# Another order of work around the last head of an attention and in the first block of a Strassen MLP

## The chip, the cores and the metric

The kernel runs on one core of a Trainium2 chip. The metric is the device time of one execution in microseconds; the median of the runs is given. The engines are called TensorE (PE, with PEld for its weight loads), VectorE (DVE), ScalarE (ACT), GpSimd (POOL) and SyncE (SP). Here SyncE issues all large DMAs, in order: a wait of one DMA holds back all that are written behind it.

## The reference, cut to what matters

One layer of a transformer on 2048 rows of 1024 numbers in f32: differential attention with 8 heads, then an MLP of width 4096 with a squared ReLU.

```python
u = rms_norm(h, norm1_g)
q, k, v = split(u @ w_in, 3)                      # 8 heads, two maps of width 64 each, v of width 128
p = softmax(where(mask, q @ k.T * scale, -inf))   # for both maps; chunk-causal mask
pd = p[:, :, 0] - lam * p[:, :, 1]
o = rms_norm(pd @ v, sub_g) * (1 - lambda_init)
h = h + o @ w_out
u = rms_norm(h, norm2_g)
h = h + square(relu(u @ mlp_w1)) @ mlp_w2
```

## The kernel before

All products are made from f32 numbers split into a high part (f32r) and a low part, three matmuls for each product. There are three stages.

The attention is 128 steps, a = 0 to 127: head h = a // 16, row block j = a % 16 of 128 rows. A step makes the scores of block a, turns (transposes) the probabilities of block a - 1 and multiplies them with v. Up to head 6 it also projects q, k and v of block a + 16. In the last head no projection is left; its place is taken by the output product. Step j there works on output tile t = j - 4: it multiplies the turned attention outputs of row block t with w_out (`pe_product(t, d, parts)`: two column halves d, each in two parts of 12 matmuls), adds x (`dve_residual`, L821), squares the row (`act_square_h`, L829), norms it (`dve_norm_u2`, L846), turns it in the next step (`pe_turn_u2`) and splits it into the seven factors of the MLP's Strassen product. For an odd tile of a pair these are sums and differences: `turned_u2` makes two factors and the sums themselves (L940 to L949, ScalarE's copy L913), `sums_u2` the last three factors (L891 on ScalarE, L926 on VectorE). So only steps with even t have `sums_u2`, of tile t - 1. Meanwhile the outputs of row block t + 1 are loaded (`load_o`, L743), turned (`pe_turn_o`, L772) and split (`turned_o`: L780 on ScalarE, L787 on VectorE) for the next step's product.

Steps with j = 8 to 15 are written in `big_step` of each engine (t = 4 to 11 in the last head), those below in `small_step`. After step 127 a tail, written out by hand, does output tiles 12 to 15.

The order on each engine is the order in the program; engines wait for each other by semaphores. All turned blocks pass through two PSUM slots in the order of `turn_order()`. A transpose waits until its slot's last user is read (`wait_slot`). In a big step the order is u0, u1, p0, p1, ..., o0, o1, so p0 takes the slot of u0. Both halves of the output product up to tile 12 share one PSUM bank: the second half d = 1 waits for the residual of the first (`h_set`, 2t + 1).

The order of TensorE's big step in the last head is: scores of map 0, late values of block a - 2, product half 0, turned u of tile t - 1, scores of map 1, p0, half of product half 1, p1, the other half, then values and p2, p3, then the outputs of block t + 1. ScalarE's order there is: exponentials of map 0, turned u, p0, p1, exponentials of map 1 with p2 and p3 between and behind, the norm of an output, sums of u, turned outputs, square of h.

The MLP is 16 blocks: two chunks of 1024 rows by eight blocks of 512 hidden columns. A block has seven "up" products of 24 matmuls (L2102), which give the hidden values in four quarters, and seven "down" products of 24 (L2126), which are added to y (L2027). ScalarE makes the high parts of the 14 weight factors (`high_w`, L1922) and of the hidden factors (`high_a`, L1935), keeps products (`keep`, L1941), applies relu (L1947) and square (L1951). VectorE makes the low parts of w1's factors (`low_w1`, L2003) and of the hidden factors (`low_a`, L2008), and puts products together (`put_together`, L2015). GpSimd makes the low parts of w2's factors (`low_w2`, L1877) and most weight sums (`weight_sum`, L1790). Up product p = 3 waits for the first `put_together`, p = 4 for `keep` of p = 2. In the first block (`it` = 0) the last output tile's work (`last_tile`) is done between the MLP's own steps, and GpSimd's first weight sums, the first two weights' splits (`high_first_w1` L1679, `low_first_w1` L1683) lie at the end of the attention.

Of the kernel before, what the change touches and what calls it, by code (L numbers as in the profile page):

```python
# [19 lines left out]
P = 128  # L20
# [3 lines left out]
NT = S // P  # L24
# [195 lines left out]
def attention_engines(nc, ctx, x, norm1_g, w_in, q_g, k_g, lambdas, w_out, sub_g, norm2_g, o_dram, u_dram,  # L220
# [5 lines left out]
    def sem(name):  # L226
        return ctx.enter_context(nc.semaphore(name))
# [82 lines left out]
    def staged(pair, o, part):  # L310
# [42 lines left out]
    w_out_loaded = [sem("w_out_loaded0"), sem("w_out_loaded1")]  # L353
    w_out_hi_set, w_out_lo_set = sem("w_out_hi_set"), sem("w_out_lo_set")
    g2_loaded = sem("g2_loaded")
    o_loaded, o_turned, ot_hi_set, ot_lo_set = (
        sem("o_loaded"), sem("o_turned"), sem("ot_hi_set"), sem("ot_lo_set"))
    xr_loaded = [sem("xr_loaded0"), sem("xr_loaded1")]
    multiplied, h_set, h_squared = sem("multiplied"), sem("h_set"), sem("h_squared")
    h_var_set, h_rs_set, u2_normed, u2_turned = (  # L360
# [366 lines left out]
    def low_w_out(engine, kt):  # L727
        engine.wait_ge(w_out_hi_set, kt + 1)
        engine.tensor_tensor(w_out_lo[:, kt, :], w_out_raw[:, kt, :], w_out_hi[:, kt, :].bitcast(F32),
                             ALU.subtract).then_inc(w_out_lo_set, 1)  # L730

    def load_o(sp, t):
        if t == 0:
            for n in range(4):
                sp.wait_ge(w_lo_set[n], H)
            sp.wait_ge(proj_half, 2 * ALL)
            sp.dma_start(g2_row[:, :], norm2_g.to_broadcast([P, D])).then_inc(g2_loaded, 16)
        else:
            sp.wait_ge(o_turned, 2 * t)
        a = ALL - NT + t if t < NT - 2 else ALL - 2 * NT + t  # L740
        cols = slice(0, D if t < NT - 2 else D - HD)
        sp.wait_ge(o_stored[a % 2], 16 * (a // 2 + 1))
        sp.dma_start(o_in[:, cols], o_dram[t * P:(t + 1) * P, cols]).then_inc(o_loaded, 16)  # L743

    def load_x(sp, t):
        if t >= 2:
# [4 lines left out]
    def store_h(sp, t):  # L751
        sp.wait_ge(h_set, 2 * t + 2)
        sp.dma_start(h_dram[t * P:(t + 1) * P, :], xh[:, t % 2, :]).then_inc(h_stored[t % 2], 16)
# [6 lines left out]
            sp.dma_start(factor[pair % 4], stage(pair, o).bitcast(F32)).then_inc(u2_stored[STAGE[pair, o][0]], 16)  # L760

    def pe_turn_o(pe, t):
        pe.wait_ge(o_loaded, 16 * (t + 1))
        for n in range(2):
            wait_slot(pe, "o", t, n)
            for c in range(HALF):
                kt = n * HALF + c
                rows = o_in[:, kt * P:(kt + 1) * P]
                if t >= NT - 2 and kt == KT - 1:
                    pe.wait_ge(o_normed, ALL - NT + t + 1)  # L770
                    rows = o_sum[:, t % 2, :]
                last = pe.transpose(turn[:, slot_of("o", t, n), c * P:(c + 1) * P], rows, ident[:, :])  # L772
            last.then_inc(o_turned, 1)
# [182 lines left out]
    def sync(sp):  # L956
# [44 lines left out]
                store_output(sp, a - 2)  # L1001

        for t in range(NT - OUT0, NT):
            store_h(sp, t - 1)
            if t + 1 < NT:
                load_o(sp, t + 1)
            if t + 1 < NT:
                load_x(sp, t + 1)
            if t == NT - 3:
                sp.wait_ge(pv_done, groups_through(ALL - 1))  # L1010
                mlp.load_first_w1(sp)
            store_u2(sp, t - 1)
            if t == NT - 3:
                sp.wait_ge(scored, scores_through(ALL - 1))
                for place in range(11):
                    sp.wait_ge(u2_stored[place], 16 * staged_through(CT - 1, place))
                for n in range(3):
                    mlp.load_u(sp, 0, n)
            if t == NT - 2:
                for place in (0, 2, 4, 6):  # L1020
                    sp.wait_ge(u2_stored[place], 16 * STAGED[place])
                for n in range(3, 5):
                    mlp.load_u(sp, 0, n)
# [83 lines left out]
    def scalar(act):  # L1107
# [102 lines left out]
        def big_step(a, n, nb):  # L1210
            h, j = split(a)
            t = output_tile(h, j)
            np = count_of(j)
            if j > BIG:
                act_output_low(act, a - 2)
            for k in range(np):
                act_exp(act, a, 0, k)
            if n - 1 < ALL:
                act_turned_qk(act, n - 1)
            if j > BIG:  # L1220
                act_square_output(act, a - 2)
            if t >= 1:
                act_turned_u2(act, t - 1)
            if j == NT - 1 and h + 2 < H:
                act_split_weights(act, h + 2, (0, 1))
            act_turned_p(act, a - 1, 0)
            if nb > 1:
                act_turned_p(act, a - 1, 1)
            act_exp(act, a, 1, 0)
            if n < ALL:  # L1230
                act_keep_qkv(act, n)
            if nb > 2:
                act_turned_p(act, a - 1, 2)
            act_exp(act, a, 1, 1)
            if nb > 3:
                act_turned_p(act, a - 1, 3)
            if n < ALL:
                act_square_qk(act, n)
                act_v(act, n)
            act_norm_output(act, a - 2)  # L1240
            if t >= 1:
                act_sums_u2(act, t - 1)
            if j == NT - 1 and h + 2 < H:
                act_split_weights(act, h + 2, (2, 3))
            if t >= 0:
                act_turned_o(act, t + 1)
                act_square_h(act, t)

        for a in range(ALL):
# [29 lines left out]
    def vector(dve):  # L1279
# [97 lines left out]
        def big_step(a, n, nb):  # L1377
# [19 lines left out]
                dve_residual(dve, t, 1)  # L1397
            for g in range(2, nb):
                dve_turned_p(dve, a - 1, g)
            if t >= 1:  # L1400
                dve_sums_u2(dve, t - 1)
            if n < ALL:
                dve_sum_qk(dve, n)
            if t >= 0:
                dve_turned_o(dve, t + 1)
                dve_norm_u2(dve, t)

        for a in range(ALL):
# [28 lines left out]
    def tensor(pe):  # L1437
# [70 lines left out]
        def big_step(a, n, nb):  # L1508
# [10 lines left out]
            if t >= 0:  # L1519
                pe_product(pe, t, 0)  # L1520
                pe_turn_u2(pe, t - 1)
            pe_scores(pe, a, 1)
            pe_turn_p(pe, a - 1, 0)
            if n < ALL:
                pe_project(pe, n, 1, (0,))
            if t >= 0:
                pe_product(pe, t, 1, (0,))
            if nb > 1:
                pe_turn_p(pe, a - 1, 1)
            if n < ALL:  # L1530
# [156 lines left out]
def mlp_engines(nc, ctx, h_dram, w1, w2, out, at, banks, mlp, last_tile):  # L1687
# [185 lines left out]
    def gpsimd(pool):  # L1873
# [6 lines left out]
        def body(b, it, chunk, first):  # L1880
# [2 lines left out]
                for name in SUMS_OF_W1:  # L1883
                    weight_sum(pool, it, 0, name)
            low_w2(it, 0)
            weight_sum(pool, it, 1, "t2")
            low_w2(it, 1)
            weight_sum(pool, it, 1, "t4")
            low_w2(it, 2)
            low_w2(it, 3)  # L1890
# [11 lines left out]
    def scalar(act):  # L1902
# [50 lines left out]
        def body(b, it, chunk, first):  # L1953
# [1 line left out]
                high_w(it, 2)  # L1955
            high_w(it, 3)
            keep(it, 0, a11)
            if static(it, 0):
                last_tile.act_turned(act)
            high_w(it, 4)  # L1960
            if static(it, 0):
                last_tile.act_sums(act)
            high_w(it, 5)
            high_w(it, 6)
            square(it, C11, a11)
            high_a(it, 0)
            keep(it, 2, a12)
            if not static(it, 0):
# [31 lines left out]
    def vector(dve):  # L2000
# [28 lines left out]
        def body(b, it, chunk, first):  # L2029
            if static(it, 0):  # L2030
                low_w1(it, 2)
            low_w1(it, 3)
            if static(it, 0):
                last_tile.dve_turned(dve)
            low_w1(it, 4)
            if static(it, 0):
                last_tile.dve_sums(dve)
            if not static(it, 0):
                weight_sum(dve, it, 1, "t1")
                weight_sum(dve, it, 1, "t3")  # L2040
            put_together(it, X0, 1, a11)
            low_w1(it, 5)
            low_a(it, 0)
            low_w1(it, 6)
            put_together(it, Y3, 4, a22)
            put_together(it, X2, 5, a12)
            low_a(it, 1)
            if static(it, 0):
                weight_sum(dve, it, 1, "t1")
                weight_sum(dve, it, 1, "t3")  # L2050
            dve.wait_ge(hid_set, it * 4 + C21)
            dve.wait_ge(a_lo_set, it * NP + 1)
            dve.tensor_tensor(a11, a11, a21, ALU.subtract).then_inc(s_set, 1)
# [162 lines left out]
```

## Time and profile before

| | us |
|---|---|
| median of 3 runs | 2846.42 (2845.59 to 2848.49) |
| the profiled execution | 2845.15 |
| its span, first to last instruction | 2843.4 |
| TensorE busy | 2736.3 (96%), mean granted clock 0.990 |
| VectorE busy | 1899.5 (67%) |
| ScalarE busy | 1504.2 (53%) |
| GpSimd busy | 1081.3 (38%) |
| steps with projections end | 1236 |
| last head's big steps | 1353 to 1531 |
| tail (tiles 12 to 15) | 1532 to 1603 |
| first MLP product | 1603.45 |

Of the execution's time, 1.8 us lie outside the span. The granted clock is a share of full speed: 1.00 is 2.4 GHz, 0.50 is 1.2 GHz. A matmul's duration in the trace is longer than its distance to the next, since matmuls are pipelined; distances are the better measure.

### The profile page before, as it was taken

The numbers are of one execution on the slowest core, as the hardware profiler recorded it, in microseconds if no ns is written. First come the engines' busy times: TensorE is split into PE (matmuls) and PEld (weight loads), VectorE is DVE, ScalarE is ACT, GpSimd is POOL, SyncE is SP. The second block draws the span as 40 slices with busy tenths as digits, with TensorE's granted clock in tenths as the row PEclk, the third lists the DMA queues.
The fourth block names the chain that finished last, engine by engine and source line by source line (L and its number), as shares of the span: only waits on it lengthen the run. The fifth ranks groups of instructions, "written<-read, shape, count | busy, mean of one in ns | idle before, by whom it ended". The sixth has DMA issues, their size and how long they took to land. (4 is left out here: it accounts for less than half of the span.)

```text
span 2843.4 us, 42848 instructions
## 1 busy us (share of the span) xinstructions
PE 2736.3 (96%) x14784; PEld 2374.4 (84%) x14784; DVE 1899.5 (67%) x2726; ACT 1504.2 (53%) x2987; POOL 1081.3 (38%) x956
## 2 busy tenths in 40 slices
PE   7999999999999999979899899999999999999999
PEld 7898989889898989867777678888888888888887
DVE  6777787777777777765676566555555556666655
ACT  5666666666666666664454334444444444444443
POOL 5633334243333425241001254444444444444443
PEclk9999999999999999989999999999999999999999
DMA  7742424243242424224444986666666876666663
GB/s 261 263 138 88 156 95 161 88 144 111 97 147 95 152 92 142 81 94 147 155 163 158 354 301 239 264 265 245 257 266 266 324 287 237 234 240 239 238 239 133
DMA packets 181808, 544.09 MB, mean 191 GB/s; under 512 B 14736, under 2 KB 88208, under 8 KB 136592
## 3 DMA queue, kind: packets, MB, share of 16 engines
q1 hardware_dynamic: 180608, 541.91, 52.2%
q8 instruction: 90, 1.47, 0.2%
q14 instruction: 70, 0.57, 0.1%
q10 hardware_dynamic: 1040, 0.13, 0.0%
HBM read 470.81 MB, written 71.17 MB: 191 GB/s over the span
## 5 line engine op out<-in xcount | busy, mean ns | idle before, releaser
L2102 PE MATMUL banks<-u,w 128*128 128x512 f32 x2688 | 614.3, 390 | 5.1 <-issue 5.1
L417 PE MATMUL banks<-w_hi,u_ring 128*128 128x384 f32 x2048 | 589.6, 348 | 11.9 <-DVE w_lo L396 4.8
L2102 PEld LDWEIGHTS banks<-u,w 128*128 128x128 f32 x2688 | 505.8, 188 | 110.6 <-issue 5.5
L2126 PE MATMUL banks<-w,a_hi 128*128 128x512 f32 x1792 | 553.1, 390 | 5.2 <-POOL w L1877 4.2
L1877 POOL TENSOR_TENSOR w<-w_raw,w 128x1024 fp32r<-128x1024 f32 x96 | 247.1, 2587 | 544.7 <-ACT w L1922 274.2
L601 ACT ACTIVATE p_all<-banks,bias 128x1024 f32<-128x1024 f32 (+7 forms) x384 | 330.8, 864 | 135.7 <-DVE bias L581 67.7
L2126 PEld LDWEIGHTS banks<-w,a_hi 128*128 128x128 f32 x1792 | 337.0, 188 | 76.1 <-POOL w L1877 4.6
L417 PEld LDWEIGHTS banks<-w_hi,u_ring 128*128 128x128 f32 x2048 | 376.2, 189 | 16.7 <-issue 10.7
L2126 PE MATMUL banks<-w,a_lo 128*128 128x512 f32 x896 | 349.3, 390 | 0.0
L447 POOL TENSOR_TENSOR qk_rs<-qk_var,minus_half 128x4 f32<-128x4 f32 x128 | 129.4, 1011 | 573.6 <-DVE qk_var L441 573.6
L417 PE MATMUL banks<-w_lo,u_ring 128*128 128x384 f32 x1024 | 344.8, 337 | 0.0
L649 DVE TENSOR_TENSOR pt_lo<-banks,pt_hi 128x512 fp32r<-128x512 f32 (+2 forms) x320 | 190.5, 608 | 182.5 <-ACT pt_hi L643 182.1
L662 PE MATMUL banks<-v_s,pt_hi 128*128 128x256 f32 x1088 | 282.5, 337 | 30.4 <-DVE pt_lo L649 20.4
L2027 DVE TENSOR_TENSOR y<-banks,y 128x1024 f32<-128x1024 f32 x224 | 267.4, 1218 | 48.1 <-PE banks L2126 46.9
L1922 ACT ACTIVATE w<-w_raw 128x1024 fp32r<-128x1024 f32 x190 | 197.7, 1050 | 177.3 <-PE banks L2102 89.8
L643 ACT ACTIVATE pt_hi<-banks 128x512 fp32r<-128x512 f32 (+2 forms) x320 | 170.2, 532 | 199.5 <-PE banks L634 199.4
L559 PE MATMUL banks<-k_s,q_hi 128*128 128x512 f32 (+3 forms) x640 | 254.3, 400 | 2.7 <-ACT p_all L601 2.7
L578 DVE TENSOR_REDUCE mx<-banks 128x1 f32<-128x1024 f32 (+7 forms) x256 | 246.1, 985 | 12.2 <-PE banks L561 10.5
L662 PEld LDWEIGHTS banks<-v_s,pt_hi 128*128 128x128 f32 x1088 | 206.8, 190 | 49.9 <-issue 36.3
L664 PE MATMUL banks<-v_s,pt_lo 128*128 128x128 f32 x1088 | 243.3, 224 | 0.0
L561 PE MATMUL banks<-k_s,q_lo 128*128 128x512 f32 (+3 forms) x640 | 232.6, 368 | 0.0
L1935 ACT ACTIVATE a_hi<-hid 128x1024 fp32r<-128x1024 f32 x96 | 102.0, 1062 | 242.1 <-PE banks L2126 182.3
(149 smaller groups left out, 4743.7 us busy)
## 6 DMA issues: line engine op xcount, KB each, us to landing
u<-u_factors SPq DMA_DIRECT2D x224, 1024.0 KB, 8.7
u_ring<-u_scratch SPq DMA_DIRECT2D x112, 1024.0 KB, 5.2
w_raw<-in_mlp_w SPq DMA_DIRECT2D x128, 512.0 KB, 6.5
u_scratch<-u_ring SPq DMA_DIRECT2D x16, 1024.0 KB, 5.0
w_raw<-in_a_w_in SPq DMA_DIRECT2D x96, 128.0 KB, 4.9
u_factors<-q_hi SPq DMA_DIRECT2D x23, 512.0 KB, 3.6
u_factors<-q_lo SPq DMA_DIRECT2D x23, 512.0 KB, 3.7
p_all<-in_x SPq DMA_DIRECT2D x16, 512.0 KB, 5.7
```

What stands on the lines that cost most here:

```text
L417: last = pe.matmul(proj[:, 0:3 * HD], u[:, part, kt, :], w[:, kt, :], start=(kt == 0 and part == 0 and w is w_hi), stop=(kt == KT - 1 and ...
L559: pe.matmul(scores[:, at, 0:width], q_hi[:, m, rows], k_s[h % 2][:, m, keys], start=not masked, stop=False, skip_group_check=True)
L561: last = pe.matmul(scores[:, at, 0:width], q_lo[:, m, rows], k_s[h % 2][:, m, keys], start=False, stop=True, skip_group_check=True)
L578: dve.tensor_reduce(mx[:, m, k:k + 1], piece, AX.X, ALU.max).then_inc(piece_max, 1)
L601: act.activation(dst, flat[:, place * BANK:place * BANK + keys.stop - keys.start], ACT.Exp, bias=bias[:, par, m:m + 1], accum_out=z_part[: ...
L662: pe.matmul(o_acc[:, 0:2 * HD], pt_hi[:, g % 2, c * P:(c + 1) * P], v, start=(n == 0 and c == 0), stop=False, skip_group_check=True)
L664: last = pe.matmul(o_acc[:, 0:HD], pt_lo[:, g % 2, c * P:(c + 1) * P], v[:, 0:HD], start=False, stop=(n == nb - 1 and c == tiles - 1), ski ...
L1877: pool.tensor_tensor(weight(w, 1), full_weight(it, w), weight(w, 0).bitcast(F32), ALU.subtract)\
L1922: act.activation(weight(w, 0), full_weight(it, w), ACT.Copy).then_inc(w_hi_set, 1)
L2027: dve.tensor_tensor(part, banks[:, at:at + 2, :], part, ALU.add).then_inc(y_added, 1)
L2102: last = pe.matmul(banks[:, UP_BANKS[p] + f, :], w[:, 2 * k2 + k, f * P:(f + 1) * P], u[:, :, part, k, :], start=(STARTS[p] and k2 == 0 an ...
L2126: last = pe.matmul(banks[:, DOWN_BANKS[p] + t, :], a[:, p % 2, f, t * P:(t + 1) * P], b[:, f, :], start=(STARTS[p] and f == 0 and a is a_h ...
```

## The change

In the big steps of the last head, TensorE does the first 12 matmuls of product half 1 ahead of p0 instead of behind it. ScalarE and VectorE split the turned outputs before the sums of u instead of after them. The load of the last row block's outputs goes to a place of its own (the first half of a plane of `p_all`) with its own semaphore, and is issued at the head of the tail instead of behind tile 13's store. In the first MLP block, ScalarE squares the first hidden quarter and makes one more weight before the last tile's turned steps; VectorE puts the first quarter together before them, and makes w2's two sums before the third `put_together`; GpSimd makes the second low part of w2 before a weight sum. All other blocks keep their order.

```diff
+    def o_row(t):
+        return p_all[:, 0, 0:D] if t == NT - 1 else o_in
...
     def load_o(sp, t):
...
+        elif t < NT - 1:
+            sp.wait_ge(o_turned, 2 * t)
         else:
-            sp.wait_ge(o_turned, 2 * t)
+            sp.wait_ge(p_turned, groups_through(ALL - 2))
...
-        sp.dma_start(o_in[:, cols], o_dram[t * P:(t + 1) * P, cols]).then_inc(o_loaded, 16)
+        sp.dma_start(o_row(t)[:, cols], o_dram[t * P:(t + 1) * P, cols])\
+          .then_inc(o_last_loaded if t == NT - 1 else o_loaded, 16)
...
     def pe_turn_o(pe, t):
-        pe.wait_ge(o_loaded, 16 * (t + 1))
+        if t == NT - 1:
+            pe.wait_ge(o_last_loaded, 16)
+        else:
+            pe.wait_ge(o_loaded, 16 * (t + 1))
...
-                rows = o_in[:, kt * P:(kt + 1) * P]
+                rows = o_row(t)[:, kt * P:(kt + 1) * P]
...
         for t in range(NT - OUT0, NT):
+            if t == NT - OUT0:
+                load_o(sp, NT - 1)
             store_h(sp, t - 1)
-            if t + 1 < NT:
+            if t + 1 < NT - 1:
                 load_o(sp, t + 1)
...
             act_norm_output(act, a - 2)
+            if t >= 0:
+                act_turned_o(act, t + 1)
             if t >= 1:
                 act_sums_u2(act, t - 1)
...
             if t >= 0:
-                act_turned_o(act, t + 1)
                 act_square_h(act, t)
...
                 dve_turned_p(dve, a - 1, g)
+            if t >= 0:
+                dve_turned_o(dve, t + 1)
             if t >= 1:
                 dve_sums_u2(dve, t - 1)
...
             if t >= 0:
-                dve_turned_o(dve, t + 1)
                 dve_norm_u2(dve, t)
...
             pe_scores(pe, a, 1)
+            if t >= 0:
+                pe_product(pe, t, 1, (0,))
             pe_turn_p(pe, a - 1, 0)
             if n < ALL:
                 pe_project(pe, n, 1, (0,))
-            if t >= 0:
-                pe_product(pe, t, 1, (0,))
             if nb > 1:
                 pe_turn_p(pe, a - 1, 1)
...
             low_w2(it, 0)
-            weight_sum(pool, it, 1, "t2")
-            low_w2(it, 1)
+            if static(it, 0):
+                low_w2(it, 1)
+                weight_sum(pool, it, 1, "t2")
+            else:
+                weight_sum(pool, it, 1, "t2")
+                low_w2(it, 1)
...
             keep(it, 0, a11)
-            if static(it, 0):
-                last_tile.act_turned(act)
             high_w(it, 4)
             if static(it, 0):
+                square(it, C11, a11)
+                high_w(it, 5)
+                last_tile.act_turned(act)
                 last_tile.act_sums(act)
-            high_w(it, 5)
-            high_w(it, 6)
-            square(it, C11, a11)
+                high_w(it, 6)
+            else:
+                high_w(it, 5)
+                high_w(it, 6)
+                square(it, C11, a11)
             high_a(it, 0)
...
             if static(it, 0):
+                put_together(it, X0, 1, a11)
+                low_w1(it, 4)
                 last_tile.dve_turned(dve)
-            low_w1(it, 4)
-            if static(it, 0):
+                low_w1(it, 5)
                 last_tile.dve_sums(dve)
-            if not static(it, 0):
+            else:
+                low_w1(it, 4)
                 weight_sum(dve, it, 1, "t1")
                 weight_sum(dve, it, 1, "t3")
-            put_together(it, X0, 1, a11)
-            low_w1(it, 5)
+                put_together(it, X0, 1, a11)
+                low_w1(it, 5)
             low_a(it, 0)
             low_w1(it, 6)
             put_together(it, Y3, 4, a22)
+            if static(it, 0):
+                last_tile.wait_rows(dve)
+                weight_sum(dve, it, 1, "t1")
+                weight_sum(dve, it, 1, "t3")
             put_together(it, X2, 5, a12)
             low_a(it, 1)
-            if static(it, 0):
-                weight_sum(dve, it, 1, "t1")
-                weight_sum(dve, it, 1, "t3")
```

## Rows read from the trace of the kernel before

**Rows 1.** Chain that ended last, in time order: start us, us, what
```profile
1627.05 18.44 PE banks L2102 x72
...
1674.35 22.01 PE banks L2126 x96
1696.35 38.08 PE banks L2102 x168
```

**Rows 2.** TensorE's waits, 1236 to 1610 us: total us, times, longest us
```profile
PE banks L634 <- ACT qk_nat L913: 9.4, 5, 2.6
PE banks L772 <- DMA o_in<-rows_scratch: 5.7, 1, 5.7
```

**Rows 3.** Windows: length, busy us by engine, then granted clock, DMA share, GB/s
```profile
1404.80:1412.84 8.04, 7.99 (x32) 6.53 (x33) 4.33 (x8) 1.75 (x4) 0.00 (x0) 0.79 0.35 130
1427.84:1434.34 6.50, 6.41 (x32) 5.40 (x33) 3.87 (x6) 2.10 (x5) 0.00 (x0) 1.00 0.46 173
...
1584.10:1596.20 12.10, 12.02 (x44) 9.76 (x44) 6.61 (x7) 5.98 (x9) 5.49 (x4) 0.76 0.80 274
...
1632.00:1639.00 7.00, 7.00 (x33) 5.78 (x32) 0.62 (x1) 2.92 (x3) 2.31 (x1) 1.00 1.02 414
```

**Rows 4.** TensorE in time order, last head: start us, us, work [idle before <-releaser]
```profile
1402.54 0.39 PE L561 MATMUL banks<-k_s,q_lo 128*128 128x512 f32 x1
1404.85 0.41 PE L634 MATMUL banks<-ident,p_all 128*128 128x128 f32 x2 [1.93 <-ACT qk_nat L913]
...
1419.74 0.50 PE L811 MATMUL banks<-w_out_hi,ot_hi 128*128 128x512 f32 x1 [1.94 <-DVE ot_lo L787]
...
1496.97 0.41 PE L634 MATMUL banks<-ident,p_all 128*128 128x128 f32 x2 [1.40 <-ACT qk_nat L913]
```

**Rows 5.** VectorE and ScalarE in time order, steps t = 6 and 7
```profile
1401.40 0.68 DVE L821 TENSOR_TENSOR xh<-banks,xh 128x512 f32<-128x512 f32 x1
...
1418.28 1.40 DVE L787 SCALAR_TENSOR_TENSOR ot_lo<-banks,g_o,ot_hi 128x512 fp32r<-128x512 f32 x2
...
1426.29 0.68 DVE L821 TENSOR_TENSOR xh<-banks,xh 128x512 f32<-128x512 f32 x1
...
1415.81 0.63 ACT L891 ACTIVATE q_lo<-rows 128x512 fp32r<-128x512 f32 x1
...
1417.37 1.26 ACT L780 ACTIVATE ot_hi<-banks,g_o 128x512 fp32r<-128x512 f32 x2
```

**Rows 6.** TensorE, SyncE, VectorE and GpSimd in time order, tail; y's load
```profile
1584.16 1.76 PE L772 MATMUL banks<-ident,o_in 128*128 128x128 f32 x7 [5.68 <-DMA o_in<-rows_scratch]
...
1597.04 0.66 PE L861 MATMUL banks<-ident,u_nat 128*128 128x128 f32 x4 [0.86 <-DVE u_nat L846]
...
1570.60 0.38 SPq L743 DMA_DIRECT2D o_in<-rows_scratch  x1
...
1645.59 2.31 SPq L1815 DMA_DIRECT2D y<-rows_scratch  x4
...
1572.26 1.28 DVE L846 SCALAR_TENSOR_TENSOR u_nat<-xh,h_rs,g_row 128x1024 f32<-128x1024 f32 x1 [2.11 <-POOL h_rs L839]
...
1593.59 3.40 DVE L846 SCALAR_TENSOR_TENSOR u_nat<-xh,h_rs,g_row 128x1024 f32<-128x1024 f32 x1 [2.12 <-POOL h_rs L839]
...
1593.52 2.38 POOL L1683 TENSOR_TENSOR w<-w_raw,w 128x1024 fp32r<-128x1024 f32 x1
```

**Rows 7.** VectorE, ScalarE and GpSimd in time order, first MLP block
```profile
1615.46 3.42 DVE L2003 TENSOR_TENSOR w<-first_t,w 128x1024 fp32r<-128x1024 f32 x1
...
1625.73 1.22 DVE L2015 TENSOR_TENSOR hid<-banks,hid 128x1024 f32<-128x1024 f32 x1
...
1673.04 1.21 DVE L2008 TENSOR_TENSOR a_lo<-hid,a_hi 128x1024 fp32r<-128x1024 f32 x1
...
1630.13 1.00 ACT L1941 ACTIVATE hid<-banks 128x1024 f32<-128x1024 f32 x1
...
1657.14 3.34 POOL L1877 TENSOR_TENSOR w<-w_raw,w 128x1024 fp32r<-128x1024 f32 x1
```

More of the change, by code:

```diff
@@ L355, in attention_engines @@
     g2_loaded = sem("g2_loaded")
-    o_loaded, o_turned, ot_hi_set, ot_lo_set = (
-        sem("o_loaded"), sem("o_turned"), sem("ot_hi_set"), sem("ot_lo_set"))
+    o_loaded, o_last_loaded, o_turned, ot_hi_set, ot_lo_set = (
+        sem("o_loaded"), sem("o_last_loaded"), sem("o_turned"), sem("ot_hi_set"), sem("ot_lo_set"))
     xr_loaded = [sem("xr_loaded0"), sem("xr_loaded1")]
```

## The prediction

> **What bounds the kernel now.** Three views, in this order. First the chain of work that ended last: from 1674 us on it is nothing but TensorE matmuls, 38.1 us for every 168 of them, with no other engine between them [rows 1]. So whatever is saved before 1674 us is kept to the end, and nothing can be saved after it. Second the waits of TensorE between the projections' end and the MLP [rows 2]: the reader sees 9.4 us of transposes of probabilities that wait for ScalarE's line 913 and 5.7 us for the load of an attention output row block. Third the windows, for the granted clock [rows 3]: a stretch with 32 matmuls that follows a stall takes 8.04 us at a granted clock of 0.79, the same work without a stall 6.50 us at 1.00. The product's matmuls after the longest stall take 0.63 us each and start 0.43 us apart, against 0.39 and 0.23 elsewhere: the lower of the two levels (1.2 GHz) instead of 2.4. A stall therefore costs its own length and something behind it.
>
> All times below are on the clock of the trace of before; t is the output tile, p the Strassen product of the MLP's block.
>
> **Part 1, product ahead of the turned probabilities (eight steps, t = 4 to 11).** In a step with even t, TensorE finishes its scores at 1402.93 and waits 1.93 us for the transposes [rows 4]. Their PSUM slot is freed by ScalarE's copy L913, which follows VectorE's combine, residual and two differences. Behind the stall 12 product matmuls stand, and they need only the residual of the first half, L821, which ended at 1402.08 [rows 5]. Put first, they run about 3.0 us (12 x 0.227 plus the last one's tail) and cover the whole wait. From the end of the scores to the first values matmul this step takes 9.9 us (1402.93 to 1412.84 [rows 3, 4]), a step without a stall 6.5 [rows 3]: 3.4 us saved. The same happens four times, and the stalls are 1.35, 1.93, 2.13 and 1.40 us (four in all; the second and the last are in [rows 4]); the two of about 2 us lose another 1.5 us to the clock, the two short ones nothing. Sum 1.3 + 3.4 + 3.6 + 1.3 = 9.6 us. What is late next: the low part of the first transposed group. VectorE reaches it after its two row maxima in either order, at 1407.8, and values would start at 1409.7, so there is still a microsecond. The two transposes now stand back to back, so the exponentials of the second map are released no later than before.
>
> In a step with odd t the transposes hardly wait (0.1 to 0.3 us), and the product's new place has a condition that the transposes had not: L821 must be over. In the step of t = 7 it ends at 1426.97 [rows 5]. Before, scores end at 1427.84, so it costs nothing; but see part 2. I take 0.1 us saved in each of the odd steps, between a loss of 0.9 and a gain of 0.3.
>
> **Part 2, turned outputs ahead of u's sums.** Only steps with even t have sums. ScalarE begins three sum copies at 1415.8 and reaches the turned outputs at 1417.37, though TensorE had turned them by 1415.87; VectorE's L787 follows at 1418.28, and TensorE's product waits 1.94 us [rows 4, 5]. Exchanged, L787 ends about 1.7 us sooner. Of the four such steps this stall is 0, 1.94, 0.84 and 0 us, so 2.6 us of gain are offered. The sums themselves (3 x 0.52 us on ScalarE, 3 x 0.6 on VectorE) then lie ahead of the square of h either way, when ScalarE is late anyway: the norm, the next maxima, the combine and L821 stay where they were, or come up to 1.4 us later in the two steps where ScalarE had been early. So the next odd step's product half, which now needs L821, waits for it: TensorE comes 1.7 us sooner and waits 0.9 us more. I count 0.5 + 0.3 us of the 2.6. Ends for this part: -1.5 (L821 late by 1.4 us in two steps, with nothing won) to 2.6. Last head in all: 9.6 (even steps) + 0.4 (odd steps) + 0.8 (this part) - 1.0 (a third of the 3 us of slow clock, should other short waits keep it) = 9.8 us, between 5 and 12.
>
> **Part 3, the last output row block's load.** It is issued at 1570.60 behind three megabyte loads, and TensorE waits 5.68 us for it at 1584.16 [rows 6]. It moves to some 40 us earlier, ahead of the store of h's tile 11 and the load of block 13, on the in-order SP queue; its wait (probabilities of the tile before the last all turned) is over by then, since TensorE's last such transpose is at 1528.6 and the SP queue stands behind a later event. Block 13 is needed at 1553.6; nothing is delayed. With the stall goes the slow clock behind it: 1584.10 to 1596.20 takes 12.1 us for 8 transposes and 36 products that need 9.3 at the full rate (36 x 0.227 + 1.1), so 5.7 + 2.8 = 8.5 us at the end of that product. Late next: the norm of tile 14, through ScalarE. ScalarE copies two MLP weights (L1679) before it squares h, VectorE's norm L846 takes 3.40 us there instead of 1.28 because GpSimd's L1683 runs beside it, and TensorE waits 0.86 us for it [rows 6]. Rebuilt with ScalarE's queue (outputs to 1580.2, sums 1581.8, two copies 1583.7, square 1584.8, two small GpSimd steps 1586.1, norm 1589.5), TensorE would be there at 1587.6 and waits 1.9 us. The gain is 7.5 us (1597.04 against 1589.5), between 5 and 8.5; the following steps keep it.
>
> **Part 4, the MLP's first block.** p = 3 begins at 1627.05, 5.1 us late, when VectorE's L2015 (first sum of hidden values) ends [rows 1, 7]. L2015 stood behind the last tile's six turned steps, two weight low parts and three sums; it now stands right behind L2003, which ends at 1618.88, so it ends at 1620.1, before TensorE is through with p = 2 (1621.9). The 5.1 us stall goes. Late next: p = 4 needs ScalarE's copy L1941, at 1630.13 before. ScalarE's new order puts relu, square, one weight, three turned copies (a ping-pong with VectorE, 2.0 us), three sums (2.4), a weight and a_hi ahead of it: 1620.2 + 2.1 + 1.0 + 2.0 + 2.4 + 1.0 + 1.0 = 1629.7, and the copy itself ends at 1630.8 (full tiles 1.05 us, half tiles 0.6 [rows 5, 7]). TensorE wants it at 1627.4: a new stall of 3.4 us, with 1.3 us of clock behind it as in part 1. Then the down products: p = 1 waited 4.2 us for GpSimd's L1877 at 1657.14, which stood behind a weight sum of VectorE; in the new order it needs only two weights and is done by 1638, so this stall goes. The next in line is the low part of a for down p = 3, L2008 at 1673.04, which let TensorE go on at 1674.35 [rows 1, 7]. Its chain (last hidden square 1650.6, two differences beside GpSimd 1655.1, a_hi 1656.2, low part 1659.1, two adds, two sums, two adds, low part 1667.1) ends 7.1 us sooner. Less some clock behind its stall of 2.3 us: 6.5 us, between 3 and 8.
>
> *A rule weighed.* VectorE's norm takes 1.28 us alone and 3.40 beside GpSimd [rows 6]. The Trainium skill, page "SBUF — State Buffer", section "SBUF: two separate sides", says why: the two share one pair of ports, held for a whole instruction, and the other blocks. The change brings VectorE's two weight sums near GpSimd's L1877 of p = 1. By that rule, if they met, each sum would take some 3.4 us, ScalarE's queue would stand behind them and part 4 would give 3 us instead of 6.5. By the times above they follow each other, and I leave it out.
>
> **Sum.** 9.8 + 7.5 + 6.5 = 23.8 us. The profiled execution took 2845.15 us, so 2821.3; the median of the runs is 1.3 us above that execution: 2822.6 us.
>
> **The rivals.**
> DMA takes over. The engines' share is 0.94 to 1.07 from 1562 to 1583 and 1.00 and more from 1611 to 1639 (one of these windows is in [rows 3]), and the u factors, the MLP's weights and y all pass there. The changed order asks for the same bytes in 14 us less, and the idle DMA time between 1583 and 1646 is about 7 us. For it: y's load was issued at 1645.6 [rows 6] and is wanted at 1659 in my schedule. Against: no matmul waited for a load in the MLP. It would leave 9.8 + 7 = 17 us: 2829.6.
> The residual takes the place of the transposes. If L821 came after the scores in even steps too, the 9.6 us would shrink to about 3: 2829.2. For: in t = 8 it ends only 0.65 us before the scores. Against: it moves with the steps before it.
> Slower. Every transpose of a step's first group comes 3.0 us later relative to the scores, and exponentials, combine and L821 of the next step stand behind it. Were that loop the bound and not TensorE, each of eight steps would lose up to 3.0 us plus 1.5 us of clock: 36 us against the 14 us of parts 3 and 4 and none from part 1, so 2868; it decides once L821 is more than 1.8 us a step later than the scores, when 8 steps eat the 14. Nothing in the odd steps points to it, since the second group's transpose, not the first, releases the exponentials.
> It does nothing: the load of the row block only gives way to the load of x's last tile, issued at 1583, and the MLP's stall moves whole to p = 4, with the last head's gain lost in L821: 2846.
>
> **How the numbers follow.** Forecast 0.64; DMA 0.16; residual 0.12; slower 0.04; nothing 0.04. Low end: all offered gains taken, 12 + 8.5 + 8 = 28.5, so 2818, and 2 us for a clock that stays up. High end: both partial rivals, 2830, and room for them together, 2834. About 5.7 us (0.2%) is what a measurement of this kernel can tell from no change; the first three cases are all beyond it: faster 0.92, same 0.04, slower 0.04.
>
> **What would show it.** No wait of a transpose for L913 in t = 4 to 10; no wait for the o_in load; L2015 ending before p = 2 does; a new wait of some 3 us at p = 4 for L1941; the uninterrupted matmuls beginning near 1650 instead of 1674. It is wrong if product matmuls show waits for L821 over 1 us in most steps, or if MLP matmuls wait for a DMA.

## The result and the profile after

The changed kernel takes 2828.06 us (median of 4 runs, 2827.03 to 2828.83) against 2846.01 (4 runs, 2844.37 to 2848.49): the ratio is 0.9936, 95% interval 0.9919 to 0.9953. It is faster by 18 us; 23.8 were forecast. The profiled execution took 2827.03 us, its span is 2825.2. Lines behind L360 have moved by some numbers: the product is L821 now, the residual L831, turned outputs L797, ScalarE's copy L923, up products L2126, down products L2150, the adds L2048, `put_together` L2036.

Where the time went is read best from four marks on TensorE: the start of the product of t = 4 (first big step), of t = 12 (tail), of the first up product, and of the second block's first.

| us | to t = 4 | head | tail | first block | rest | span |
|---|---|---|---|---|---|---|
| before | 1355.69 | 177.12 | 70.64 | 92.74 | 1147.21 | 2843.4 |
| changed | 1357.15 | 164.60 | 61.95 | 93.92 | 1147.58 | 2825.2 |
| difference | +1.5 | -12.5 | -8.7 | +1.2 | +0.4 | -18.2 |

The way to t = 4 is the same code in both; it varied from 1355.7 to 1360.9 us over all the kernels below, so a difference of 1.5 us there can't be put down to the change.

TensorE's waits in the head of the changed kernel (us in total, times, longest); the 6.8 us for L913 are gone (4 of the 5 waits in [rows 2]; the fifth, 2.6 us, is in the tail and stays), and 1.4 us for the residual L831 are new:

```profile
PE banks L782 <- DVE pt_lo L649: 2.1, 5, 0.6
PE banks L821 <- DVE ot_lo L797: 1.8, 3, 1.2
PE banks L821 <- DVE xh L831: 1.4, 3, 0.7
```

The step of t = 6, TensorE in order of time, which answers to [rows 4]: the product follows the scores without a gap, and the eight transposes stand together behind it.

```profile
1402.45 0.39 PE L561 MATMUL banks<-k_s,q_lo 128*128 128x512 f32 x1
1402.68 0.40 PE L821 MATMUL banks<-w_out_hi,ot_hi 128*128 128x512 f32 x1
...
1405.18 0.39 PE L821 MATMUL banks<-w_out_hi,ot_lo 128*128 128x512 f32 x1
1405.41 1.03 PE L634 MATMUL banks<-ident,p_all 128*128 128x128 f32 x8
...
1409.02 0.28 PE L662 MATMUL banks<-v_s,pt_hi 128*128 128x256 f32 x1
```

TensorE's waits in the changed kernel's first MLP block and just before:

```profile
PE banks L2150 <- DVE y L2048: 7.2, 1, 7.2
PE banks L2126 <- issue: 2.6, 1, 2.6
PE banks L2126 <- DMA u<-u_factors: 0.7, 2, 0.5
```

And its chain that ended last, around the longest of them. Before, this stretch of the chain was work of VectorE, ScalarE, GpSimd and TensorE; now it is two DMAs, the store of the last tile's factors and the load of y:

```profile
1617.17 16.14 DMA u_factors<-y_stage
1634.89 11.61 DMA y<-rows_scratch
1648.09 29.69 PE banks L2150 x120
1677.78 38.08 PE banks L2126 x168
```

VectorE in the same stretch, in order of time (it waits 6.65 us; the adds before had not waited for y), and the windows of that time (length, busy us by engine, granted clock, DMA share, GB/s):

```profile
1637.92 2.16 DVE L2029 TENSOR_TENSOR a_lo<-s,a_hi 128x1024 fp32r<-128x1024 f32 x1 [1.19 <-ACT a_hi L1953]
1646.72 2.36 DVE L2048 TENSOR_TENSOR y<-banks,y 128x1024 f32<-128x1024 f32 x2 [6.65 <-DMA y<-rows_scratch]
```
```profile
1597.00:1625.00 28.00, 24.71 (x100) 19.33 (x99) 19.51 (x19) 14.31 (x17) 6.43 (x4) 0.94 1.02 414
1639.00:1667.00 28.00, 20.76 (x83) 16.66 (x82) 19.46 (x15) 5.14 (x6) 11.50 (x4) 0.88 1.05 400
```

So the stalls of 5.1, 4.2 and 1.0 us in the block are gone, and 7.2, 2.6 and 0.7 us have taken their place.

### The profile page after: what moved, and what is told of

It reads as the page before. It is cut to its first block, busy times and chain, and to the rows that moved or that the text cites. A ratio compares the mean times of both kernels' runs of the same rounds, so it can differ in the third digit from the quotient of the medians.

```text
span 2825.2 us, 42849 instructions
## 1 busy us (share of the span) xinstructions
PE 2730.3 (97%) x14784; PEld 2368.7 (84%) x14784; DVE 1899.1 (67%) x2726; ACT 1504.8 (53%) x2987; POOL 1077.9 (38%) x956
## 4 chain that ended last, share of the span: by engine, by line
PE 70%; DVE 14%; issue 7%; ACT 4%; DMA 3%; POOL 1%; SPq 1%; ACTq 0%; DVEq 0%; POOLq 0%
PE banks L2150 21%; PE banks L2126 21%; PE banks L417 11%; DVE mx L578 5%; PE banks L662 4%; PE banks L821 3%; DVE p_all L623 3%; PE banks L634 3%; PE banks L559 2%; PE banks L561 2%; PE banks L664 1%; ACT p_all L601 1%; ACT pt_hi L643 1%; PE banks L509 1%; DVE pt_lo L649 1%
## 5 line engine op out<-in xcount | busy, mean ns | idle before, releaser
L2126 PE MATMUL banks<-u,w 128*128 128x512 f32 x2688 | 614.9, 390 | 3.3 <-issue 2.6
L2126 PEld LDWEIGHTS banks<-u,w 128*128 128x128 f32 x2688 | 505.3, 188 | 109.9 <-issue 3.9
L2150 PE MATMUL banks<-w,a_hi 128*128 128x512 f32 x1792 | 553.8, 390 | 7.2 <-DVE y L2048 7.2
L2150 PEld LDWEIGHTS banks<-w,a_hi 128*128 128x128 f32 x1792 | 337.3, 188 | 78.0 <-issue 7.6
L2150 PE MATMUL banks<-w,a_lo 128*128 128x512 f32 x896 | 349.5, 390 | 0.0
L2048 DVE TENSOR_TENSOR y<-banks,y 128x1024 f32<-128x1024 f32 x224 | 267.5, 1219 | 54.3 <-PE banks L2150 46.4
```

Of the source, the lines that this page charges most:

```text
L2048: dve.tensor_tensor(part, banks[:, at:at + 2, :], part, ALU.add).then_inc(y_added, 1)
L2126: last = pe.matmul(banks[:, UP_BANKS[p] + f, :], w[:, 2 * k2 + k, f * P:(f + 1) * P], u[:, :, part, k, :], start=(STARTS[p] and k2 == 0 an ...
L2150: last = pe.matmul(banks[:, DOWN_BANKS[p] + t, :], a[:, p % 2, f, t * P:(t + 1) * P], b[:, f, :], start=(STARTS[p] and f == 0 and a is a_h ...
```

## The experiments

Nine kernels. The marks are those of the table above; y's load is given as the time of its issue behind the start of t = 12's product. Ratios are against the kernel before, timed anew beside each group of kernels. Marks and waits come from one profiled execution of each kernel.

| kernel | median us | ratio, 95% interval | head | tail | block | y's load at |
|---|---|---|---|---|---|---|
| before | 2846 to 2847 | | 177.12 | 70.64 | 92.74 | 112.8 |
| changed | 2828.06 | 0.9936, 0.9919 to 0.9953 | 164.60 | 61.95 | 93.92 | 111.6 |
| part 1 alone | 2835.34 | 0.9962, 0.9948 to 0.9975 | 164.55 | 69.56 | 92.79 | 111.9 |
| part 2 alone | 2847.14 | 1.0002, 0.9993 to 1.0011 | 175.24 | 70.82 | 92.69 | 113.2 |
| part 3 alone | 2840.01 | 0.9976, 0.9967 to 0.9985 | 174.08 | 63.50 | 93.53 | 112.4 |
| part 4 alone | 2839.66 | 0.9976, 0.9967 to 0.9985 | 177.05 | 70.83 | 85.95 | 113.4 |
| parts 1, 2, 3 | 2827.58 | 0.9931, 0.9917 to 0.9944 | 164.67 | 63.10 | 93.05 | 112.8 |
| y by quarters | 2823.28 | 0.9920, 0.9907 to 0.9934 | 164.57 | 62.96 | 86.19 | 112.3 |
| store before u | 2828.03 | 0.9933, 0.9919 to 0.9946 | 164.53 | 61.98 | 95.66 | 107.4 |
| fewer bytes | 2821.45 | 0.9907, 0.9891 to 0.9924 | 164.56 | 63.42 | 86.95 | 106.7 |
| further order | 2819.81 | 0.9909, 0.9894 to 0.9924 | 164.56 | 58.31 | 89.77 | 109.5 |

**Part 1 alone.** The kernel before with only TensorE's big step changed:

```diff
             pe_scores(pe, a, 1)
+            if t >= 0:
+                pe_product(pe, t, 1, (0,))
             pe_turn_p(pe, a - 1, 0)
...
-            if t >= 0:
-                pe_product(pe, t, 1, (0,))
```

> The kernel before with part 1 alone: in the last head's big steps TensorE does 12 matmuls of product half 1 ahead of the first turned probabilities. Theory (the transposes' wait for L913 is covered): from the product of t = 4 to that of t = 12, which took 177.1 us before and 164.6 after the whole change, this takes about 167.5, with the waits of the product for L787 (1.9 and 0.8 us) left; 9.5 us faster in all. Rival (the residual L821 takes the transposes' place): waits of 1 us or more for L821 in the even steps and at most 3 us saved.

The head took 164.55 us, 12.6 less. Its waits:

```profile
PE banks L811 <- DVE ot_lo L787: 4.4, 4, 1.9
PE banks L772 <- DVE pt_lo L649: 2.1, 5, 0.6
```

No wait for L913 and none for the residual: the transposes' wait was covered in full, and the rival falls. The head is 3.0 us shorter than the 167.5 expected; its gain is 2.6 us more than part 1's term, and all of the head's gain in the changed kernel.

**Part 2 alone.** The two exchanges of `turned_o` and `sums_u2` on ScalarE and VectorE, in the kernel before.

> The kernel before with part 2 alone: turned outputs ahead of u's sums in the last head's big steps. Part 1 alone took the head (product of t = 4 to that of t = 12) from 177.1 to 164.55 us, the whole change to 164.60, so part 2 gave nothing there. Theory (the product comes sooner, but VectorE's chain to L821 and the combine does not, so the next wait grows by the same): the waits for L787 fall from 1.9 and 0.8 us to under 0.3, and the wait for L913 or the combine behind them grows; head 175 to 177 us. Rival (part 2 has a gain of its own that part 1 takes up): head 174 us or less, 3 us or more saved.

The ratio is 1.0002 and the head 175.24 us, both as the theory says. TensorE in order of time: the product waits 0.19 us where it had waited 1.94 [rows 4], and the next transposes, which had not waited, now wait 1.51 us for VectorE's L926, behind the residual. Another wait for L926, of 1.3 us, is also new.

```profile
1420.42 0.50 PE L811 MATMUL banks<-w_out_hi,ot_hi 128*128 128x512 f32 x1 [0.19 <-DVE ot_lo L787]
1430.24 0.63 PE L634 MATMUL banks<-ident,p_all 128*128 128x128 f32 x4 [1.51 <-DVE q_hi L926]
```

In the head 1.9 us are missing against the kernel before, but part 3 alone, which touches nothing there, has 3.0 less than before too. That is the clock: windows over the steps of t = 6 and t = 8, of before and then of part 3 alone, at the same stalls of 1.9 and 2.1 us:

```profile
1400.00:1420.00 20.00, 16.13 (x88) 13.37 (x88) 13.24 (x20) 10.45 (x25) 1.05 (x3) 0.91 0.25 92
1445.00:1465.00 20.00, 17.09 (x97) 14.26 (x95) 14.00 (x20) 10.81 (x25) 0.92 (x2) 0.91 0.23 83
```
```profile
1400.00:1420.00 20.00, 16.14 (x95) 13.56 (x94) 14.39 (x26) 11.37 (x25) 1.33 (x4) 1.00 0.31 117
1445.00:1465.00 20.00, 16.95 (x102) 14.18 (x101) 14.60 (x21) 10.88 (x24) 1.65 (x4) 1.00 0.31 116
```

One execution fell to a lower granted clock behind these two stalls, another did not, which is worth 1.6 + 1.5 us. Part 2 alone kept the clock at these stalls too (steps of 21.5 and 22.8 us against 24.8 and 25.4), so against part 3's 174.1 us its head is 1.2 us longer. Beside part 1 it gives nothing either: the steps with even t are 2.9 us shorter in sum and those with odd t 2.9 us longer (changed kernel 164.60, part 1 alone 164.55 us).

**Part 3 alone.** The last row block's load in its own place, issued early.

> The kernel before with part 3 alone: the last row block of outputs is loaded early into its own place. Theory: the 5.7 us wait and the slow clock behind it go, the norm of tile 14 is late by 1.8 us instead of 0.9, so the first MLP product starts 7.3 us sooner against the product of t = 12. In the MLP's first block nothing is reordered, so its own stalls (5.1, 4.2, 1.0 us) stay, and 7 us are kept to the end. Rival (the DMAs are the bound from here on): the MLP's first block grows by most of what the tail gains, and less than 3 us are left.

The tail took 63.50 us, 7.1 less (7.3 were expected), and the median fell by 7.2 us. The block took 93.53, 0.8 more: a wait of 0.5 us for u factors is new. The theory holds for the tail. But y's load, which in the kernel before was issued 42.1 us after the first up product began (1645.59 [rows 6] and 1603.45), is issued 48.9 us after it here: it did not move with TensorE. VectorE's adds now wait 1.1 us for y, which they had not done before; in the old order the adds come late, and TensorE loses nothing by it.

**Part 4 alone.** The MLP's first block in the new order, nothing else.

> The kernel before with part 4 alone: the other order in the MLP's first block. In the changed kernel this block (first MLP matmul to the next block's first) took 94.1 us against 92.9 before, with a 7.2 us wait of the adds for y's load. Theory (y's load is late because the compressed tail and this block ask the DMAs for the same bytes in less time): here the tail is not compressed, so y's load is some 3 to 5 us less late, and the block takes 88 to 90 us, 3 to 5 us faster. Rival (the new order itself holds y's stores and its load back): the same 7 us wait, 93 to 95 us, nothing saved.

The block took 85.95 us, 6.8 less, and the median fell by 7.6 us; 88 to 90 us and a gain of 3 to 5 had been expected. TensorE's waits there:

```profile
PE banks L2112 <- issue: 3.1, 1, 3.1
PE banks L2136 <- DVE y L2034: 1.3, 1, 1.3
PE banks L2136 <- issue: 1.0, 1, 1.0
```

The wait for y's adds is 1.3 us where the changed kernel has 7.2. The new order is good for what was forecast, as long as the tail is not shortened. But it has no room left: the chain that ended last already runs through the last factor store and y's load, and VectorE's first add waits for y.

```profile
1630.36 16.05 DMA u_factors<-y_stage
1647.99 11.61 DMA y<-rows_scratch
```
```profile
1659.82 2.35 DVE L2034 TENSOR_TENSOR y<-banks,y 128x1024 f32<-128x1024 f32 x2 [0.66 <-DMA y<-rows_scratch]
```

**Parts 1, 2 and 3 with the old block.**

> The changed kernel with part 4 undone: the MLP's first block in the old order. Theory (part 4, worth 6.8 us alone, was lost to y's late load once the tail was shortened): the block takes 92.5 to 94 us, as in the changed kernel (93.9), and the total is the changed kernel's, 2827 to 2829. Rival (part 4 still gives its own, and the changed kernel lost the time elsewhere): 5 to 7 us slower than the changed kernel, 2833 or more.

The block took 93.05 us and the whole 2827.58, the changed kernel's time. With part 3 in place and y awaited as a whole, part 4 gives nothing; the rival falls. In this kernel too VectorE's adds wait for y, 2.7 us, though they come later.

**y by quarters.** In the changed kernel each add waits for its own quarter of y:

```diff
-            if first:
-                for q in LAST_ADDED:
-                    dve.wait_ge(y_loaded[q], 16 * (chunk + 1))
             for p in range(NP):
+                if first and ADDED_BEFORE[p] is None:
+                    dve.wait_ge(y_loaded[QUARTER_OF_Y[p]], 16 * (chunk + 1))
                 add(it, p, 0)
```

> The changed kernel, where each add waits only for its own quarter of y instead of the first add for all four. Theory (the 11.6 us of y's load are what the adds wait for): the first quarter is there some 7 us sooner, the adds start at about 1640 us instead of 1646.7, down p = 2 no longer waits, a wait of about 2 us at down p = 3 is left, and it is 5 to 6.5 us faster than the changed kernel (2822 to 2823). Rival (VectorE's own queue of adds and low parts sets down p = 3): at most 1 us faster.

2823.28 us, 4.8 less than the changed kernel where 5 to 6.5 were expected, and the block 86.19 instead of 93.92. VectorE in order of time; the adds follow the low part without a wait:

```profile
1639.42 2.16 DVE L2029 TENSOR_TENSOR a_lo<-s,a_hi 128x1024 fp32r<-128x1024 f32 x1 [1.19 <-ACT a_hi L1953]
1641.51 2.34 DVE L2048 TENSOR_TENSOR y<-banks,y 128x1024 f32<-128x1024 f32 x2
```

So the adds' wait for y was what took part 4's gain, and VectorE's own queue was not: TensorE's waits at down p = 2 and p = 3 are 0.5 and 1.1 us. That makes part 4's gain visible again: against the old order behind the same parts 1 to 3 (93.05 us) the block is 6.9 us shorter.

**Store before u.** In the changed kernel SyncE issues the last tile's factor stores ahead of the block's last two u loads.

```diff
             for n in range(NP, 2 * NP):
+                if static(it, 0) and n == NP + 5:
+                    last_tile.store(sp)
```

> The changed kernel, where SyncE issues the last tile's five factor stores (2.5 MB) ahead of the last two u loads of the block (2 MB) instead of behind them. Theory (y's load waits for the stores to land, and these stand in a full DMA queue behind the u loads): the stores land about 4 us sooner, y's load too, and the adds' wait of 7.2 us falls to 3 to 4; against it, the two u loads come later and up p = 6 waits 1 to 3 us for them; 1 to 3 us faster. Rival (the stores are slow for another reason, the queue's order does not matter): y lands at the same time and the block grows by the waits of p = 6.

y's load came 4.3 us sooner, as expected, and the wait for its adds fell from 7.2 to 0.5 us, more than expected. The price was far above the expectation of 1 to 3 us:

```profile
PE banks L2127 <- DMA u<-u_factors: 10.8, 2, 9.7
PE banks L2127 <- issue: 1.7, 1, 1.7
PE banks L2151 <- issue: 1.1, 1, 1.1
PE banks L2151 <- DVE y L2049: 0.5, 1, 0.5
```

Up p = 6 waited 9.7 us for its factors, the block grew by 1.7 us, and the median, 2828.03, is the changed kernel's: nothing was saved. The queue's order decides who is late, not whether something is late, which speaks for the transfers as the bound.

**Fewer bytes.** The direct test of that.

```diff
+                if static(it, 0) and n >= 2 * NP - 3:
+                    mlp.load_u(sp, chunk, n, P)
+                else:
+                    mlp.load_u(sp, chunk, n)
```

> The changed kernel, where the last three u loads of the MLP's first block bring only a sixteenth of their megabyte (2.8 MB less; the rest of these factors is left out, so the products of that block are computed from the factors that were there). In five kernels y's load was issued 111.6 to 113.4 us after the product of t = 12 began, whatever TensorE did in between. Theory (the DMAs set this time): 2.8 MB less at the 410 GB/s of this stretch bring y's load 6 to 7 us sooner, 105 to 106 us after that point, the adds' wait of 7.2 us falls below 1 and the block takes 86 to 88 us instead of 93.9; 6 to 8 us faster than the changed kernel, about 2821. Rival (a fixed latency of the stores, or SyncE's waits on semaphores, sets it): y's load stays at 111 us or later and less than 2 us are saved.

y's load was issued 106.7 us behind t = 12's product, 4.9 sooner than in the changed kernel and 5 to 7 sooner than in all kernels with the full bytes in the same order. The block took 86.95 us and the median fell by 6.6 us to 2821.45. TensorE still waits 3.6 us for the adds, where under 1 was expected:

```profile
PE banks L2153 <- DVE y L2051: 3.6, 1, 3.6
PE banks L2129 <- DMA u<-u_factors: 1.6, 1, 1.6
```

The median is where it was expected. The theory stands, but y's load came 1 to 2 us less early than forecast, and the wait for the adds fell by 3.6 us instead of more than 6.

**Further order.** y by quarters, and two edits of the tail:

```diff
+        pe_product(pe, t, 1, (0,))
         pe_turn_p(pe, last, 0)
         pe_turn_p(pe, last, 1)
-        pe_product(pe, t, 1, (0,))
...
+            act_square_h(act, t)
             if t == NT - 2:
                 mlp.high_first_w1(act)
-            act_square_h(act, t)
...
             pool_factor_h(pool, t)
-            if t >= NT - 3:
-                mlp.low_first_w1(pool, t - NT + 3)
+        for n in range(2):
+            mlp.low_first_w1(pool, n)
```

> y by quarters as before, and two further edits in the tail: 12 matmuls of product half 1 of tile 12 stand ahead of the last block's turned probabilities, and tile 14's square and factor come ahead of the first two MLP weights' splits on ScalarE and GpSimd. Theory: the wait of 2.6 us for L913 in the tail is covered, the norm of tile 14 takes 1.3 us instead of 3.4 because GpSimd is not beside it, and TensorE waits for neither; the tail takes 57 to 58.5 us instead of 62 to 63, the block 86 to 88, so 2819 to 2821, 2 to 4 us faster than y by quarters alone. Rival (the DMAs bound what follows): the tail is shorter, but the block takes 90 us or more and nothing is kept.

The tail took 58.31 us, as expected, 4.6 less than y by quarters alone. The norm of tile 14 took 1.28 us, and TensorE waited neither for it nor for L913. But the block took 89.77, 3.6 more than in y by quarters and 2 more than expected. It waits longer for u factors, and 2.0 us for the norm of tile 15, the last one (L856):

```profile
PE banks L2125 <- DMA u<-u_factors: 4.8, 2, 3.1
PE banks L871 <- DVE u_nat L856: 2.0, 1, 2.0
```

In the two profiled executions about 1 of the 4.6 us is kept, which is nearer to the rival. The medians differ by 3.5 us, which is inside the theory's 2 to 4, but the intervals of the two ratios overlap. So these two edits give something between 1 and 3.5 us, and the runs don't settle where. At 2819.81 us it is the lowest median of a kernel here that computes everything, 0.9909 of the kernel before.

## Why the prediction was right or wrong

The time lies in the range and the direction is right; for the profiled execution the sum was 5.7 us too large. That is 7.7 us too much for the first block, less 2.7 too little for the head and 1.2 too little for the tail, and 1.9 us that the stretches with the same code took longer. So the sum owes part of its closeness to errors that cancel.

*Part 1 (10.0 us forecast, 1.0 taken off again).* Measured 12.6. The mechanism is as forecast: no wait for L913 in t = 4 to 10, and no wait for the residual in the even steps. Two sizes were off. The deduction for slow clock was wrong: 3.1 us of the kernel before's head are slow clock behind the two longer stalls, in its profiled execution, and they all went. And the steps gave about 0.24 us each beyond their waits: (12.6 - 3.1 - 6.8 - 0.8) / 8, the 6.8 and 0.8 being the waits of transposes. The product begins before the scores' modelled end (1402.68 against 1402.84), where the transposes of a step without a stall began after theirs (1427.93 against 1427.84). That this is where the 0.24 us come from is an inference; no run isolates it.

*Part 2 (0.8 us forecast, 2.6 offered).* Measured nothing. The step was right that VectorE's chain to the residual would hold TensorE in the next step; it gave back the whole, not two thirds.

*Part 3 (7.5 us).* Measured 8.7 in the changed kernel and 7.1 alone. The last row block's wait is gone, and the next wait is the one named, the norm of tile 14, with 1.8 us (1.9 forecast). The 1.6 us between the two kernels are mostly the step of t = 12, whose stall of 2.62 us stayed in both: 22.3 us at a granted clock of 1.00 in the changed kernel, 23.9 at 0.93 with part 3 alone. They are the clock's and not part 3's, so about 7.1 is what part 3 gives.

*Part 4 (6.5 us).* This is the step that failed. Alone it gave 6.8, with 3.1 us of stall at p = 4 where 3.4 were named. In the changed kernel the block took 1.2 us more than before. The sum took y to be there when VectorE's adds were ready and put that wait at nothing. In its place TensorE waited 7.2 us for the adds, and these waited 6.65 us for y. Three kernels show that this wait took the gain: part 4 alone (6.8 us gained), the old order behind parts 1 to 3 (nothing lost), and y by quarters (6.9 us gained against that).

The prediction's own times held the error. In the kernel before, the four loads of y were issued from 1645.6 to 1647.1 us, and the last took 11.6 us to land, so y was there at 1658.7. The adds of the new order were put behind a low part that ends at 1659.1. That is no room at all, and on a clock that does not yet contain part 3. With its 7.5 us the adds are ready at 1651.6, about 7 us ahead of y, if y's load stays where it was. The rival's "for" compared the load's issue, not its landing, with the adds, and left part 3's shift out.

That rival, the DMAs take over, got a chance of 0.16 and the time 2829.6 us. It is what happened, and its time is 1.5 us off, partly by luck: it had 9.8 us for the head where 12.5 were measured. Its evidence was in the trace: DMA shares about 1.0, with y issued only behind stores that wait in the same queue. The argument against it ("no matmul waited for a load") spoke of a schedule in which the DMAs had 14 us more.

The signs that the prediction named do not tell the two apart. TensorE waited no more at up p = 3, waited 2.6 us at p = 4 (3 named), and ran without a stop from 1648.1 us (1650 named), but with 120 down matmuls still to do where 96 were left before. Only the sign against it came true in small: up products waited 0.7 us for a DMA, u's factors.

What was not seen is how stiff this is. In eight kernels that move the same bytes, and in the same order from the u loads on, y's load was issued 111.6 to 113.4 us behind t = 12's product, while TensorE reached the first up product after 62 to 71 us. The last tile's factor stores, which y's load waits for, were issued from 99.5 us behind that mark in the kernel before and from 89.3 in the changed kernel, 10 us earlier, and the load came only 1.1 us earlier. The gain of part 3 moves TensorE, not the transfers. It is not quite rigid: with a tail of 58.3 us (further order) the load was issued at 109.5.

The rule of the Trainium skill that the prediction weighed (page "SBUF — State Buffer", section "SBUF: two separate sides") agrees with the trace, and bore most on another place than the one named. Tile 14's norm took 3.39 us in the changed kernel, begun 0.06 us behind GpSimd's operation, and 1.28 in the further order, begun 0.10 us ahead of it. Both engines in those two cases, changed kernel first:

```profile
1573.85 3.39 DVE L856 SCALAR_TENSOR_TENSOR u_nat<-xh,h_rs,g_row 128x1024 f32<-128x1024 f32 x1 [2.62 <-POOL h_rs L849]
...
1573.79 2.37 POOL L1697 TENSOR_TENSOR w<-w_raw,w 128x1024 fp32r<-128x1024 f32 x1
```
```profile
1571.59 1.28 DVE L856 SCALAR_TENSOR_TENSOR u_nat<-xh,h_rs,g_row 128x1024 f32<-128x1024 f32 x1 [2.11 <-POOL h_rs L849]
...
1571.69 5.79 POOL L1697 TENSOR_TENSOR w<-w_raw,w 128x1024 fp32r<-128x1024 f32 x2
```

Whoever comes second waits: in the second case GpSimd's two operations took 5.79 us, 1.05 more than twice the 2.37 of the first. One of VectorE's two weight sums in part 4 did meet GpSimd (2.74 us instead of 1.23), which cost nothing, since y was later.

What stays open: the bytes were cut by 2.8 MB in one kernel only, which leaves parts of three u factors out, and not in one that computes everything. So how much of the remaining 10 us of the first block (86.2 against 76.2 for a later one) is the transfers' is not shown.

## What to carry to other kernels

Where the DMAs are at a share of 1.0, a stall of TensorE that is removed does not move the transfers behind it: add up the bytes between there and the first load that is issued behind a store, and date that load by the bytes, not by the engines. An operand that arrives in parts should be waited for in parts; that alone gave back 5 us here. Two edits that each give 7 us alone can give 7 together when they lead to the same transfer, so the last term of a sum needs its own check against what the earlier terms have moved.

## What the runs showed of the hardware that was not expected

The same stall costs different time in different executions. Behind stalls of 1.9 and 2.1 us the granted clock over 20 us was 0.91 in the profiled executions of the kernel before and of part 4 alone (steps of 24.8 and 25.3 us) and 1.00 in those of part 3 alone and part 2 alone (23.2 and 23.8 for part 3). Behind the stall of 2.6 us at t = 12 the step had 1.00 in the changed kernel and 0.93 with part 3 alone.

And SyncE can be held in issuing a DMA. It took 11.9 us to issue five stores of 0.5 MB in the changed kernel, from 1611.06 on, against 2.5 us in the kernel before, from 1632.28 on, so that every wait written behind them comes late too. The DMA share does not tell the two apart: it was 1.03 in the first stretch and 1.02 in the second. What differs is how much had been issued just ahead. The changed kernel had issued 11 MB of loads in the 16 us before; in the kernel before, SyncE had waited for TensorE to free places of u (17.5 us in five waits from 1600 to 1650 us, 4.3 in the changed kernel from 1590 to 1640). With 2.8 MB less in those loads (fewer bytes) the same five stores took 5.7 us. That the transfers still outstanding hold SyncE is the reading that fits these three numbers; it was not tested by itself.
